# Head reordered, and both layer norms done by token halves, in a two-block float32 network kernel

## What is computed

```python
def layer_norm(x, g, b):
    mu = jnp.mean(x, axis=-1, keepdims=True)
    var = jnp.mean(jnp.square(x - mu), axis=-1, keepdims=True)
    return ((x - mu) * lax.rsqrt(var + LN_EPS)) * g + b

def modulation(cond, w, b, n):
    m = jax.nn.silu(cond) @ w[:, :n * D_MODEL] + b[:n * D_MODEL]
    return jnp.split(m, n, axis=-1)

# layer i of the first block (i = 0: even_mixer, i = 1: odd_mixer)
sh, sc, gt = modulation(c_lat, w_ada[i], b_ada[i], 3)
u = x * (1.0 + sc) + sh
sh_c, sc_c = modulation(c_c, w_ada[i], b_ada[i], 2)     # i = 0, for the context rows
s_f, s_b = context_states((ctx * (1.0 + sc_c) + sh_c) @ w_in_e[:, :E_STATE_COLS], ...)
y = even_mixer(u @ w_in_e, s_f, s_b, ...) or odd_mixer(u @ w_in_o, w_pool, pool_scale, w_out_o, ...)
x = layer_norm(alpha * x + gt * y, ln_g[i], ln_b[i])

# second block, cross-attention keys and values (the kernel makes the keys first of all)
k, v = split_cols(rms_norm(mem, norm_mem) @ w_kv_cross, ...)
```

## Time and profile before

| what | value |
|---|---|
| median of 3 runs | 2410.95 us (2410.42 to 2413.95) |
| profiled execution | 2408.33 us, its span 2406.5 us |
| PE busy | 2351.4 us, 98% of the span |
| DVE, ACT, POOL busy | 1442.4, 1094.7, 70.6 us |
| idle of PE for the memory rows, at the start | 10.1 us |
| idle of PE at the two layer norms | 8.9 us |
| idle of PE for conditioning weights | 4.1 us |

### The profile page before, as it was taken

The page is one execution under the profiler, slowest core; times in us unless marked ns, Lnnn a source line. Parts: engine busy times, 40 slices in busy tenths (PEclk is TensorE's granted clock), DMA queues, the critical chain, the costliest instruction groups (busy, mean ns, idle before and its releaser), DMA issues.

```text
span 2406.5 us, 30234 instructions
## 1 busy us (share of the span) xinstructions
PE 2351.4 (98%) x12212; PEld 1912.5 (79%) x12212; DVE 1442.4 (60%) x1416; ACT 1094.7 (45%) x1147; POOL 70.6 (3%) x116
## 2 busy tenths in 40 slices
PE   7999999999999999999999989999999999999998
PEld 5667887887678788887878877788888888888886
DVE  3445477755956887567667685665545545445454
ACT  4322554544653534546555352455544334334333
POOL 1000001000000000000000000000000000000000
PEclk9999999999999999999999999999999999999999
DMA  9994578856965697555545311754665565565563
GB/s 370 321 332 154 180 248 281 266 169 248 385 221 187 228 367 237 203 191 157 193 140 177 103 30 42 270 183 149 185 183 184 192 192 175 201 192 182 194 210 123
DMA packets 234022, 496.07 MB, mean 206 GB/s; under 512 B 21568, under 2 KB 23680, under 8 KB 226848
## 3 DMA queue, kind: packets, MB, share of 16 engines
q1 hardware_dynamic: 221360, 438.99, 55.2%
q0 software_dynamic: 11984, 54.13, 6.1%
q10 hardware_dynamic: 544, 1.05, 0.1%
HBM read 487.84 MB, written 6.29 MB: 205 GB/s over the span
## 4 chain that ended last, share of the span: by engine, by line
PE 68%; DVE 5%; ACT 1%; issue 1%; DVEq 0%; ACTq 0%
PE banks L2950 61%; PE banks L3023 2%; PE banks L3391 1%; PE banks L3289 1%; PE banks L3486 1%; DVE decayed_a L2032 0%; DVE inverse_products L2642 0%; PE banks L3380 0%; PE banks L2927 0%; DVE inverse_by_chunk L2643 0%; PE banks L3286 0%; DVE decayed_b L2032 0%; DVE scores_diag L2057 0%; PE banks L3660 0%; DVE decayed_a L2041 0%
## 5 line engine op out<-in xcount | busy, mean ns | idle before, releaser
L1717 DVE TENSOR_TENSOR weights_lo<-weights_raw,weights_hi 128x2048 fp32r<-128x2048 f32 x348 | 795.3, 2286 | 686.2 <-ACT weights_hi L862 676.6
L862 ACT ACTIVATE weights_hi<-weights_raw 128x2048 fp32r<-128x2048 f32 x348 | 665.6, 1913 | 884.2 <-PE banks L2950 811.5
L2950 PE MATMUL banks<-weights_hi,acts_hi 128*128 128x512 f32 (+1 forms) x2032 | 514.2, 395 | 2.6 <-DVE latent_keys L1879 1.4
L2950 PE MATMUL banks<-weights_hi,acts_lo 128*128 128x512 f32 (+1 forms) x2032 | 501.3, 389 | 0.0
L2950 PE MATMUL banks<-weights_lo,acts_hi 128*128 128x512 f32 (+1 forms) x2032 | 500.2, 388 | 0.0
L2950 PEld LDWEIGHTS banks<-weights_hi,acts_hi 128*128 128x128 f32 x2032 | 377.1, 189 | 88.3 <-issue 11.5
L2950 PEld LDWEIGHTS banks<-weights_hi,acts_lo 128*128 128x128 f32 x2032 | 382.0, 188 | 79.0
L2950 PEld LDWEIGHTS banks<-weights_lo,acts_hi 128*128 128x128 f32 x2032 | 380.8, 188 | 78.0
L2950 PE MATMUL banks<-weights_hi,hidden_hi 128*128 128x512 f32 x288 | 71.5, 390 | 0.0
L2950 PE MATMUL banks<-weights_lo,hidden_hi 128*128 128x512 f32 x288 | 71.1, 389 | 0.0
L2950 PE MATMUL banks<-weights_hi,hidden_lo 128*128 128x512 f32 x288 | 71.1, 389 | 0.0
(11 more groups left out here) (614 smaller groups left out, 2270.7 us busy)
## 6 DMA issues: line engine op xcount, KB each, us to landing
weights_raw<-in_w_in_e SPq DMA_DIRECT2D x72, 1024.0 KB, 5.5
weights_raw<-in_w_up SPq DMA_DIRECT2D x64, 1024.0 KB, 5.5
weights_raw<-in_w_down SPq DMA_DIRECT2D x64, 1024.0 KB, 5.1
weights_raw<-in_w_in SPq DMA_DIRECT2D x44, 1024.0 KB, 5.0
modulation_weights<-in_w_ada SPq DMA_DIRECT2D x64, 512.0 KB, 10.8
raw_eight<-in_w_ada SPq DMA_DIRECT2D x32, 1024.0 KB, 8.5
weights_raw<-in_w_in_o SPq DMA_DIRECT2D x32, 1024.0 KB, 5.4
gate_piece<-in_w_ada POOLq DMA_DIRECT2D x32, 512.0 KB, 5.5
```

Of the source, the lines that this page charges most:

```text
L862: eng.activation(WHI[:, c % 2, :, 0:n], RAW[:, sl, :, 0:n], ACT.Copy).then_inc(hi_ready, 1)
L1717: eng.tensor_tensor(WLO[:, c % 2, :, 0:n], RAW[:, c % 4, :, 0:n], WHI[:, c % 2, :, 0:n].bitcast(F32), ALU.subtract).then_inc(lo_ready, 1)
L2950: ins = eng.matmul(BANKS[:, par * 2 + h, 0:s.n], x[:, kt + k, h * P:(h + 1) * P], w[:, c % 2, k, 0:s.n], start=(kc == 0 and k == 0 and m = ...
```

## The change

It has four parts. (1) In the head, SP asks for constants and columns first, instead of POOL; the memory rows come in four column quarters of 512 KB, in between the `mem_k` and conditioning chunks, and PE waits for each quarter alone. (2) Three more places for conditioning chunks (one lies in what is later `rank_weights_hi`, two in the upper halves of `acts_hi` and `acts_lo`) are used by chunks 12 to 14, 19 and 20; POOL puts the load of the rank weights behind the fourteenth conditioning chunk. (3) `ada0` has no padding block, so `mem_k` runs on banks 2 and 3, the first conditioning sums on bank 0, and `ctx_kv` begins on 0 and 1 and ends on 2 and 3. (4) Both norms go by token halves: PE runs the upper half of the last two chunks first (`last_by_half`), then the lower; ACT normalises the upper half (`upper_norm`), DVE the lower; the tile jobs are four rows of features by 128 tokens, and chunks 0 and 1 of the next product go by half (`first_by_half`).

The diff, cut to its core:

```diff
+    CONDX = [place(f"modulation_weights_{n}", kb, [P, 4, NB]) for n, kb in enumerate((167.5, 87.5, 103.5))]
-        s.pad = 0 if s.name in ("lora", "cross_q", "mem_k") else (b + s.units) % 2
+        s.pad = 0 if s.name in ("ada0", "lora", "cross_q", "mem_k") else (b + s.units) % 2
-    COND_BANK = (2, 7, 5, 7)
-    MEM_LOADS = {1: 2, 3: 3}
+    COND_BANK = (0, 7, 5, 7)
+    MEM_BLOCKS = {0: 2, 2: 3}
+    MEM_LOADS = {2: 2, 5: 3}
+    COND_SLOT = [0, 1, 2, 3] * 3 + [4, 5, 6] + [0, 1, 2, 3, 5, 6] + [0, 1, 2, 3] * 2 + [0, 1, 2]
+    HALF_TILES = [(0, 0), (1, 0), (0, 1), (1, 1), (2, 0), (2, 1), (3, 0), (3, 1)]
...
             if s.own_ring:
-                memory(MEM0)
+                eng.dma_start(CONST[:, 0:COMMON], a["common_consts"]).then_inc(S("consts_in"), 16)
+                eng.dma_start(COLS[:, :], a["cols"]).then_inc(S("cols_in"), 16)
                 for c in range(2):
+                    memory(MEM0, (c,))
                     load(st["mem_k"], 0, c, c)
                 for m in range(s.kc * s.nblk):
-                    if m >= 4:
-                        eng.wait_ge(S("cond_used"), m - 3)
+                    if COND_LAST[m] is not None:
+                        eng.wait_ge(S("cond_used"), COND_LAST[m] + 1)
+                    elif COND_SLOT[m] > 4:
+                        eng.wait_ge(chunk_used, st["mem_k"].g0 + 4 + 2)
...
+                    if m in MEM_BLOCKS:
+                        memory(MEM0, (MEM_BLOCKS[m],))
...
     @block.gpsimd
-        eng.dma_start(COLS[:, :], a["cols"]).then_inc(S("cols_in"), 16)
-        eng.dma_start(CONST[:, 0:COMMON], a["common_consts"]).then_inc(S("consts_in"), 16)
...
+        eng.wait_ge(S("cond_used"), 14)
...
     @block.scalar
+        def upper_norm(b):
+            eng.activation(XN[:, b, 0, :], XN[:, b, 0, :], ACT.Identity, scale=STAT[:, 66:67], bias=STAT[:, 67:68])\
+               .then_inc(S("act_rows"), 1)
+        def normed_hi(name, *tiles):
+            for pos in tiles:
...
+                for i in range(4):
+                    f = 4 * b + i
+                    ins = eng.activation(normed_tile(k)[:, i, :], bank(jj)[:, i * P:(i + 1) * P], ACT.Identity,
+                                         scale=NORMC[:, 0, f:f + 1], bias=NORMC[:, 1, f:f + 1])
...
+                eng.activation(half_tile(XTH, b, h), normed_tile(k), ACT.Copy).then_inc(S("tile_hi"), 1)
+        def residual_norm(name):
+            def steps(second_hi):
+                root(STAT[:, 66:67])
+                roots[0] += 1
+                eng.wait_ge(S("square_in"), roots[0])
+                upper_norm(0)
+                second_hi()
+                upper_norm(1)
+                normed_hi(name, 0)
+                root(STAT[:, 70:71])
+                normed_hi(name, 1)
+                upper_norm(2)
+                upper_norm(3)
-        root(STAT[:, 66:67])
-        root(STAT[:, 70:71])
-        stream(st["in_o"], after={1: normed_hi("x1T", 1, 0, 1, 2), 2: normed_hi("x1T", 1, 3), ...
+        stream(st["in_o"], after={1: lambda: normed_hi("x1T", 2, 3), 2: lambda: normed_hi("x1T", 4, 5), 3: lambda: normed_hi("x1T", 6, 7), ...
...
     @block.vector
+        def upper_scale():
+            ch.link(eng.reciprocal(rstd, rstd))
+            ch.add(eng.tensor_scalar(STAT[:, 67:68], mean, rstd, -1.0, ALU.mult, ALU.mult))
+            ch.done("square_in")
...
+                    if h == 0:
+                        upper_scale()
+                        lo(following, following.g0, 0, 0)
...
+        def normed_acts(name, s):
+            normed_lo(name, 0)
+            lower_norm(0)
             lo(s, s.g0, 0, 1)
+            normed_lo(name, 1)
+            lower_norm(1, 2, 3)
+            normed_lo(name, 2, 3)
...
     @block.tensor
+        def first_by_half(s):
...
+            normed_tiles(name, 0, 1)
+            eng.wait_ge(block_out, 2 * s.b0 + 2)
+            part(0, 0)
+            normed_tiles(name, 2)
+            part(1, 0)
+            normed_tiles(name, 3, 4, 5)
+            part(0, 1)
+            part(1, 1)
+            normed_tiles(name, 6, 7)
```

More of the change, by code:

```diff
@@ L881, in _, with stream @@
         held = []
-        def stream(s, each=None, after=None, hold=False, following=None):
+        def stream(s, each=None, after=None, hold=False, following=None, norm=None):
             after = after or {}
@@ new lines, in lower_norm, with normed_lo @@
+                ch.add(eng.tensor_scalar(XN[:, b, 1, :], XN[:, b, 1, :], mean, rstd, ALU.subtract, ALU.mult))
+                ch.done("block_normed")
+        def normed_lo(name, *tiles):
+            for pos in tiles:
+                b, h = HALF_TILES[pos]
+                eng.wait_ge(S("tile_hi"), CUT[name] + pos + 1)
+                eng.tensor_tensor(half_tile(XTL, b, h), normed_tile(16 * (NORMED[name] - 1) + pos),
+                                  half_tile(XTH, b, h).bitcast(F32), ALU.subtract).then_inc(S("tile_lo"), 1)
@@ new lines, in normed_tiles @@
+        def normed_tiles(name, *tiles):
+            n = NORMED[name]
+            for pos in tiles:
+                b, h = HALF_TILES[pos]
+                eng.wait_ge(*((S("block_normed"), 4 * (n - 1) + b + 1) if h else (S("act_rows"), 2 + 4 * (n - 1) + b + 1)))
+                jj = J[name] + pos
+                bank_free(eng, jj)
+                for i in range(4):
+                    ins = eng.transpose(bank(jj)[:, i * P:(i + 1) * P], XN[:, b, h, i * P:(i + 1) * P], ident)
+                full(ins, jj)
@@ L3316, in _ @@
             return
-        transposes("x1T", natural(XN), ("block_normed", 0), range(6))
         def pool_tiles(b):
@@ L3325, in pool_tiles @@
             return step
-        stream(st["in_o"], after={0: lambda: transposes("x1T", natural(XN), ("block_normed", 0), (6, 7)), 17: pool_tiles(0),
+        stream(st["in_o"], after={17: pool_tiles(0),
                                   20: pool_tiles(1), 23: pool_tiles(2), 26: pool_tiles(3)})
@@ L3342, in _ @@
             return
-        transposes("x2T", natural(XN), ("block_normed", 4), range(6))
         def index_query_tiles():
```

195 lines of the change are left out of this document (117 added, 78 removed).

## The result

| | before | changed |
|---|---|---|
| median of 20 runs | 2410.76 us (2406.55 to 2414.04) | 2416.16 us (2412.87 to 2418.22) |
| profiled execution | 2408.33 us, span 2406.5 | 2412.90 us, span 2411.1 |
| ratio of times | | 1.0021, 95% interval 1.0015 to 1.0028 |

What follows compares the result with a forecast made beforehand. PE, busy 2351.4 of 2406.5 us, was taken as the bound, so only its waits or slowing count. Terms +1.0 - .9 - 1.4 + 1.9 + 3.0 = +3.6 on 2410.95 gave 2414.5 us, range 2406.5 to 2419.5.

Steps and rivals of the forecast that it cites:

- Head, +1.0: Head up to conditioning chunk 7: bound by bytes, so PE's earlier start only moves its waits; +1.0 us.
- the latent piece: Head: all .5 MB of this load now comes ahead of conditioning chunk 7, before about .2; +.8 us.
- the small loads: Head: the two loads at the head of SP's queue add up to .3 us.
- More places, -.9: Conditioning loads no longer wait for places; PE's third wait, .92 us at 89.08, goes: -.9 us.
- Bank pair, -1.4: Start of `lat_a`: PE's 1.4 us wait for `latent_keys` goes, -1.4 us (-.5 to -1.4).
- First norm, +1.9: First norm: ACT becomes the bound; -.5 us if the clock holds, +1.9 if it falls.
- the fall of the clock: First norm: PE's idle pieces bring half clock to the upper halves of chunks 0 and 1; 6 in 10.
- Second norm, +3.0: Second norm: +.9 us with clock held, from ACT's table load in the chain, and +2.1 for the clock's fall.
- Nothing elsewhere: Later steps in `in_o` and `qi` and the later memory load lie beside PE's work: no cost.
- The clock did not hold: Rival at the norms: full clock stays, norms give -.5 and at most +.9; about 2409.5 us, chance .22.
- the start did not pay: Rival in the head: last `mem_k` chunk at full clock or fewer bytes ahead; about 2405 us, chance .12.
- The dearer tile: Rival in ACT's norm chain: small tile instructions cost over .35 us, 2417.7 at .40, 2420.9 at .45; chance .14.

Runs made afterwards that it cites:

- e2_norms: The kernel before with only the two norms by token halves (part 4): 2416.15 us, ratio 1.0024.
- e3_pair: The kernel before with only the bank pairs changed (no padding behind the first conditioning sums, bank 0): 1.71 us less in the stretch from 226 to 578 us.
- e9_shift: The kernel before with 22 needless transposes (2.4 us) on PE between the second norm and the delta stage: that stage took 4.73 us longer.
- e7_best: `e1_head` with needless transposes where PE waits, in the head, at 662 us and at both norms: 2403.66 us over 10 runs, ratio .9973.
- e1_head: The kernel before with parts 1 to 3 (head, conditioning places, bank pair) and the norms of before: 2409.68 us over 11 runs, ratio .9997.

## Why the prediction held, and where it was off

**Head, +1.0.** The mechanism is as told: bytes bound the head, and the early start turned into waits (c7 at 46.14, forecast about 46; PE's first matmul at 7.17, not 5.5). c7 starts at 45.0 to 45.2 in the four executions with the head of before and at 45.5 to 46.4, 46.1 in the mean, in the seven below. The place of the waits was wrong: ahead of c6 and c7 they come to 2.4 us in the profiled execution, not to 4 or more, and the rest stands ahead of the memory (2.57) and of c3 (1.99). Over the seven executions with this head, untouched in its loads and waits, `ctx_kv` starts -.5 to +2.8 us from before's 58.21, 1.4 in the mean; over the four with the head of before (the profiled one, `e2_norms`, `e3_pair`, `e9_shift`) 0 to 2.0, mean 1.0. So the change itself costs about .5, less than the spread between executions, and the rest is that before's profiled execution was the shortest of its four there. Off was the reason: I put .8 on the latent piece and .3 on the small loads, but the DMA moved 35 GB/s less over 10 us, .35 MB or .9 us at .39 MB per us, while the bytes landed by c7 rose from 16.4 MB by less than .2.

**More places, -.9.** -1.15, in every execution. Since the head of before, when it is late, loses that wait by itself (-.33 to -.91 in three executions), the gain against a usual execution is nearer .7.

**Bank pair, -1.4.** -1.71, the surest term.

**First norm, +1.9.** 1.1 to 3.8, 2.9 in the mean over the six executions with tiles of four instructions and no filling. The step that was off is the fall of the clock: I gave it 6 in 10 and one stretch. It came each time, in five of the six with a second stretch behind the 1.87 us ahead of chunk 2, a wait that I had listed and not priced. PE's pieces of idle were forecast well (2.0, 1.7, 2.0 and .6; 1.85, 1.50, 1.87 and .36 measured), and so was most of ACT's chain: a tile 2.1 (2.12 measured), `upper_norm` .65 (.70 to .72 from start to start), waits of ACT 2.3 (.58, 1.06, .98 and .49, together 3.1, so ACT was not almost without idle time; the .98 wasn't listed), chunk 3 at 811.22, or 811.55 without the .33 us by which this execution is ahead, where 810.1 to 812.5 was forecast.

**Second norm, +3.0.** 2.95 to 3.27, mean 3.1, in the five executions with the load in the chain: right in sum, and by luck, since two errors cancel: 1.8 with the clock held, where I had .9, and 1.3 instead of 2.1 for the fall.

**Nothing elsewhere.** This is the assumption that failed. From 664 to 690 us the same 3.2 us of idle had half clock behind it in most executions (1.5 to 3.0 us longer) and none in before's profiled one, in `e3_pair` and in `e9_shift`. Without filling, all eight executions with the head of the change have it and one of four with the head of before, 1.8 and .4 us in the mean; whether the head's shift in time brings it or chance stays open. And the delta stage took .9 to 1.2 more in the executions of the unfilled token-half norms without a delay. Part of this is in the 2.4 us between the profiled execution of before and its median, to which I had added my sum. Means of the terms, .5 - .7 - 1.7 + 2.9 + 3.1 = 4.1, leave 1.3 of the measured 5.4 for these. Against the forecast of 3.6 the errors partly cancel: head -.5, places +.2, bank pair -.3, first norm +1.0, second +.1.

**The rivals.** The clock did not hold, the start did not pay. The dearer tile fell: the Trainium skill, "ScalarE: Activation LUTs", What ACT_TABLE_LOAD costs, would by my estimate make 128 columns .39; the four instructions of a tile start .34 to .36 apart in the trace, and the tiles show 1.58 us from the first to the copy, hand-over included, near the 1.5 of the sum with .35. On the clock the Trainium skill, "TensorE: Matmul & The Clock Gate", Part 4, says that the full clock does not engage for transposes; here 37 needless transposes with 24 of the norm's behind them (`e7_best`, granted clock 1.00 from 784 to 800) kept it, so the measurement stands against the page for these float32 transposes. The trace names them MATMUL and doesn't show whether they ran in the transpose mode that the page speaks of.

## What to carry to other kernels

Before an idle stretch of PE is cut in pieces, ask which engine's chain will end the pieces: here ACT's went from two instructions a tile to four and got four normalisations on top, and the 4.46 us came back as 1.85, 1.50, 1.87 and .36, with half clock behind them. Where a wait can't be removed, useless transposes in it can be worth more than moving it: four places gave .24% (`e7_best` against `e1_head`), where parts 1 to 3 gave .03%, not clear of noise, and the token-half norms cost .24%. For effects of a few us, compare stretches between the same matmuls over several executions; one trace gave the head a gain of 3.3 us that eleven runs put at 1.3.
